# Two-block transformer layer on one core: global attention with unsplit values in the column halves and outputs kept transposed

## The reference, cut to what matters

```python
h = _rmsnorm(x, norm_gain[l])
q_a, k_a, v_a, g_a, q_b, k_b, v_b, g_b = jnp.split(h @ w_in[l], split_at, axis=-1)
...
sc = jnp.einsum('bqkgd,bskd->bkgqs', qi, k) * d ** -0.5      # 8 heads of 64, on 2 heads of keys and values
o_a = jnp.einsum('bkgqs,bskd->bqkgd', softmax(sc), v) * silu(g_a)
o_b = _neighbourhood_attn(q_b, k_b, v_b, na_rpb[l]) * silu(g_b)
x = x + jnp.concatenate([o_a, o_b], axis=-1) @ w_out[l]
```

## Time and profile before

| what | us |
|---|---|
| median of three runs | 2026.56 |
| the profiled execution's own time | 2022.47 |
| its span in the trace | 2020.7 |
| TensorE granted clock, mean | 0.989 |
| PE / DVE / ACT / POOL busy | 1900.6 / 1017.6 / 835.0 / 395.4 |
| attention a, first scores to first projection of attention b | 149.07 to 388.70 |
| attention b, pass 3 to the first matmul of wo1 | 636.9 to 672.95 |

### The profile page before, as it was taken

One profiled execution on the slowest core, in us unless ns is written; L12 is line 12 of the kernel. 1 busy time (PEld: TensorE's weight loads), 2 busy tenths in 40 slices (PEclk: granted clock), 3 DMA queues, 4 the chain that ended last, 5 costly groups with the idle time before them and its releaser, 6 DMA issues.

```text
span 2020.7 us, 39554 instructions
## 1 busy us (share of the span) xinstructions
PE 1900.6 (94%) x16369; PEld 1607.5 (80%) x16369; DVE 1017.6 (50%) x2372; ACT 835.0 (41%) x1812; POOL 395.4 (20%) x398
## 2 busy tenths in 40 slices
PE   6998899999999899989999999999999999999997
PEld 6987778888887799967777777777777788887897
DVE  4767778522444335024455544444444457775504
ACT  5336777533454324223333333334333254444423
POOL 2540000120122142222222222212112101002221
PEclk9999999999999999999999999999999999999999
DMA  5153300233323322322221122111122220004432
GB/s 177 43 176 78 83 22 1 79 92 119 108 88 102 126 74 76 109 87 62 71 75 59 54 67 66 57 59 56 56 67 62 71 58 22 22 11 156 157 136 84
DMA packets 148714, 159.96 MB, mean 79 GB/s; under 512 B 14932, under 2 KB 131992, under 8 KB 148536
## 3 DMA queue, kind: packets, MB, share of 16 engines
q1 hardware_dynamic: 148456, 156.97, 24.5%
q0 software_dynamic: 80, 0.47, 0.1%
HBM read 110.53 MB, written 52.62 MB: 81 GB/s over the span
## 4 chain that ended last, share of the span: by engine, by line
PE 70%; DVE 6%; ACT 4%; DMA 2%; issue 2%; POOL 2%; SPq 0%; DVEq 0%; POOLq 0%; ACTq 0%
PE ps L974 8%; PE ps L976 7%; PE ps L975 7%; PE ps L687 7%; PE ps L689 6%; PE ps L688 6%; PE ps L1077 4%; PE ps L1261 3%; PE ps L1284 3%; PE ps L1114 3%; PE ps L1143 2%; PE ps L1271 2%; PE ps L775 2%; PE ps L1063 1%; DMA t<-in_w_in 1%
## 5 line engine op out<-in xcount | busy, mean ns | idle before, releaser
L687 PE MATMUL ps<-t,t 128*128 128x256 f32 (+2 forms) x1392 | 434.7, 312 | 11.9 <-DVE t L2186 3.3
L688 PE MATMUL ps<-t,t 128*128 128x256 f32 (+2 forms) x1392 | 427.4, 307 | 0.0
L689 PE MATMUL ps<-t,t 128*128 128x256 f32 (+2 forms) x1392 | 427.3, 307 | 0.0
L2747 POOL TENSOR_TENSOR t<-t,t 128x512 fp32r<-128x512 f32 x183 | 237.3, 1310 | 949.7 <-ACT t L1362 949.7
L974 PE MATMUL ps<-t,t 128*128 128x512 f32 (+2 forms) x720 | 298.9, 415 | 0.8 <-ACT t L1647 0.8
L687 PEld LDWEIGHTS ps<-t,t 128*128 128x128 f32 x1392 | 268.6, 193 | 30.6 <-issue 14.4
L688 PEld LDWEIGHTS ps<-t,t 128*128 128x128 f32 x1392 | 268.8, 193 | 10.4 <-issue 0.2
L689 PEld LDWEIGHTS ps<-t,t 128*128 128x128 f32 x1392 | 268.3, 193 | 10.9
L976 PE MATMUL ps<-t,t 128*128 128x512 f32 (+2 forms) x720 | 269.6, 374 | 0.0
L975 PE MATMUL ps<-t,t 128*128 128x512 f32 (+2 forms) x720 | 269.3, 374 | 0.0
L1362 ACT ACTIVATE t<-t 128x512 fp32r<-128x512 f32 x186 | 110.1, 623 | 132.7 <-DMA t<-in_w_in 85.0
(11 more groups left out here) (262 smaller groups left out, 3212.8 us busy)
## 6 DMA issues: line engine op xcount, KB each, us to landing
t<-in_w_in SPq DMA_DIRECT2D x53, 512.0 KB, 5.8
zgate_spill<-t SPq DMA_DIRECT2D x20, 512.0 KB, 3.2
tile_bias<-t SPq DMA_DIRECT2D x16, 576.0 KB
t<-tile_bias SPq DMA_DIRECT2D x8, 1152.0 KB, 5.9
t<-in_x SPq DMA_DIRECT2D x16, 512.0 KB, 9.9
t<-zgate_spill SPq DMA_DIRECT2D x16, 512.0 KB, 3.7
feat_spill<-t SPq DMA_DIRECT2D x13, 512.0 KB, 3.3
t<-in_w_in SPq DMA_DIRECT2D x6, 1024.0 KB, 5.3
```

The lines of the kernel that those rows point to most:

```text
L687: e.matmul(dst, lh, rh, start=k == 0, stop=False)
L688: e.matmul(dst, lh, rl, start=False, stop=False)
L689: m = e.matmul(dst, ll, rh, start=False, stop=k == n - 1)
L2747: e.tensor_tensor(WLO[wslot(b)][:, o], WST[:, o], WHI[wslot(b)][:, o].bitcast(F), ALU.subtract).then_inc(w_lo.sem, w_lo.up((b, p)))
```

## The change

The items of global attention are ordered in fours: two heads by two tiles of queries. Values are no longer split: L767 of the new code multiplies the fp32 values (64 stationary columns of `QKV`) with unsplit fp32 probabilities, 256 columns of two tiles, head s in column half s. That is 16 fp32 matmuls for four items; they are issued in four parts of four, one behind each of the next four items. ACT copies one bank of turned probabilities, DVE the other. DVE multiplies the gates with 1/sum before (L2008), PE turns them (L771), ACT brings them to SBUF (`GTA`), and DVE multiplies the still transposed output with them (L2013). The result stays transposed and is written over the spent query columns of `QKV`. In pass 3 nothing is turned any more: ACT takes the high part straight from `QKV`, POOL the low part, and DVE (L2098, before ACT) takes the high part of the outputs of passes 0 to 2. Buffers of attention b move to other addresses. The banks of wo1 are written out. The second block is unchanged.

```diff
-        PTA = [[t_.rearrange("p (k c) -> p k c", c=256) for t_ in (hi_, lo_)]
-               for hi_, lo_ in ((sb([128, 2048], R, W0 + 72 * KB), sb([128, 2048], R, RW)), (WHI[0], WLO[0]))]
-        VHL = sb([128, 8, 768], R, W0 + 16 * KB)[:, :, 0:256].rearrange("p k (v s c) -> p k v s c", s=2, v=2)
-        OTA = sb([128, 256], F, W0 + 91 * KB)
+        PTA = [[sb([128, 8, 256], F, o) for o in two] for two in ((W0 + 72 * KB, RW), (RW + 8 * KB, RW + 24 * KB))]
+        GTA = sb([128, 256], F, W0 + 91 * KB)
...
-        MIXT = sb([128, 4, T], F, W0 + 16 * KB)
+        MIXT = sb([128, 4, T], F, W0)
+        GBP = [sb([128, 128], F, W0 + (18 + 3 * (t // 2)) * KB + 512 * (t % 2)) for t in range(NT)]
+        VGS = [sb([128, 256], F, W0 + (30 + 3 * i) * KB) for i in range(4)]
...
-        A_ITEMS = [(kv, h, i) for kv in range(2) for i in range(NT) for h in range(4)]
+        A_ITEMS = [(kv, 2 * g + s, 2 * i + j) for kv in range(2) for i in range(NT // 2) for g in range(2) for j in range(2) for s in range(2)]
...
+        def a_outputs(q):
+            kv, h, i = A_ITEMS[4 * q]
+            return i, tile128(2 * kv + h // 2)
+        def a_kept(n):
+            return PTA[n // 4 % 2][n % 2], tile128(n % 4 // 2)
+        def a_scored(i):
+            return 8 * (i // 2) + 5 + 2 * (i % 2)
...
+            def scores_a(n):
+                kv, h, i = A_ITEMS[n]
+                ps = [bank_at(("s", n, half), 2 * (n % 2) + half, (prob, n)) for half in range(2)]
...
                 for half in range(2):
+                    for x in range(2):
+                        m = e.matmul(ps[half], QT[:, h, tile128(i)], KTS[kv][:, x, half512(half)], start=x == 0, stop=x == 1)
+                m.then_inc(score_mm.sem, score_mm.up(n))
+            def turn_a(n):
+                w.wait_ge(*prob[n])
+                for half in range(2):
+                    ps = bank_at(("t", n, half), 4 + half, ((prob_hi, prob_lo)[half], (n, half)))
+                    for k in range(4):
+                        m = e.transpose(ps[:, tile128(k)], PB[n % 2][:, half512(half)][:, tile128(k)], ident)
+                    m.then_inc(prob_tr.sem, prob_tr.up((n, half)))
+            def value_a(q, part):
+                kv = A_ITEMS[4 * q][0]
+                i, channels = a_outputs(q)
+                ob = bank_at(("ot", q), 6, (attn_v, (q, "out"))) if part == 0 else banks[6]
+                w.wait_ge(*prob_hi[4 * q + 3, 0])
+                w.wait_ge(*prob_lo[4 * q + 3, 1])
+                w.wait_ge(*qkv_out[0, NT - 1])
+                for k in (2 * part, 2 * part + 1):
+                    for s in range(2):
+                        m = e.matmul(ob[64 * s:64 * s + 64, 0:256], QKV[:, k, 640 + 64 * kv:704 + 64 * kv], PTA[q % 2][s][:, k, :], start=k == 0, stop=k == 7)
+                if part == 3:
+                    w.wait_ge(*attn_v[q, "gates"])
+                    for j in range(2):
+                        m = e.transpose(ob[:, 256 + 128 * j:384 + 128 * j], MIXA[:, i + j, channels], ident)
+                    m.then_inc(value_mm.sem, value_mm.up(q))
+            for n in range(-1, 64 + 4):
                 i, step = n // 4, n % 4
+                if n + 1 < 64:
+                    scores_a(n + 1)
+                if 0 <= n < 64:
+                    turn_a(n)
+                if n >= 4:
+                    value_a(i - 1, step)
                 if n < 1:
                     t = n + 7
                     ps = bank_at(("ga", 1, t), t, (mixed_v, ("gate a", t)))
...
                 if 0 <= i < NT and step == 2:
-                    turn_head_keys(1, i, (6, 7))
-                elif 0 < i <= NT and step == 0:
-                    turn_head_queries(1, i - 1, (6, 7))
+                    turn_head_keys(1, i, (7,))
+                elif 1 < i <= NT + 1 and step == 0:
+                    turn_head_queries(1, i - 2, (7,))
...
-            def turn_mixed(i):
-                key = ("m", i, 0)
-                ps = bank_at(key, 7, (tile_hi, key), (tile_lo, key))
-                w.wait_ge(*attn_v[63, "out"])
...
             def output_product(n, i, ps, hi, lo):
+                w.wait_ge(*tile_hi["m", i])
                 w.wait_ge(*tile_hi["b", 3, i // 4])
                 w.wait_ge(*tile_lo["b", 3, i // 4])
-                w.wait_ge(*band_lo[2, 1])
+                w.wait_ge(*band_lo["m", NT - 1])
+                w.wait_ge(*band_lo["b", 2, 1])
...
-                    else:
-                        turn_mixed(n)
...
-                ps = bank_at(("wo1", 0, x), x, (resid_v, (0, x)))
+                ps = bank_at(("wo1", 0, x), (7, 0)[x], (resid_v, (0, x)))
...
-                    ps = bank(("wo1", n, i), ALL, (resid_v, (n, i)))
+                    ps = bank_at(("wo1", n, i), (i + 7) % 8, (resid_v, (n, i)))
...
+            w.wait_ge(*w_hi[5, 3])
+            w.wait_ge(*w_lo[5, 3])
+            for n in range(-1, 64 + 5):
+                if n >= 8 and step == 0:
+                    w.wait_ge(*value_mm[i - 2])
+                    if i > 2:
+                        w.wait_ge(*attn_v[i - 3, "out"])
+                    e.activation(GTA[:, :], psum(("ot", i - 2))[:, 256:512], ACT.Copy).then_inc(value_t.sem, value_t.up(i - 2))
+                if 0 <= n < 64:
+                    kept, tile = a_kept(n)
+                    if n > 7:
+                        w.wait_ge(*value_mm[i - 2])
+                    w.wait_ge(*prob_tr[n, 0])
+                    e.activation(kept[:, 0:4, tile], psum(("t", n, 0)).rearrange("p (k c) -> p k c", c=128), ACT.Copy).then_inc(prob_hi.sem, prob_hi.up((n, 0)))
+                if n + 1 < 64:
+                    z = n + 1
+                    w.wait_ge(*top[z])
+                    e.activation(PB[z % 2][:, :], ps_all[:, 1024 * (z % 2):1024 * (z % 2) + 1024], ACT.Exp, bias=NMX[:, z % 16:z % 16 + 1],
+                                 scale=1.0, accum_out=RSM[:, z % 16:z % 16 + 1]).then_inc(prob.sem, prob.up(z))
...
+                elif 0 < i <= NT and step == 3:
+                    split_queries(1, i - 1)
+                elif 1 < i <= NT + 1 and step == 0:
+                    head_queries(1, i - 2)
...
             def mixed_part(i):
+                w.wait_ge(*attn_v[15, "out"])
+                w.wait_ge(*dense_mm["q", 3, 1])
+                e.activation(AH[:, 0:4, tile128(i)], QKV[:, i, 0:512].rearrange("p (k c) -> p k c", c=128), ACT.Copy).then_inc(tile_hi.sem, tile_hi.up(("m", i)))
...
                         mixed_part(n)
-                        if n < len(MIXED):
-                            band_part(*MIXED[n])
                 if p < 3:
                     wt.leave()
             band_part(3, 0)
-            wt.enter()
             band_turned(B_Z + 31)
             for x in range(2):
-                wt.tick(12)
                 band_value(B_Z + 30 + x)
             band_part(3, 1)
+            wt.enter()
+            for _ in range(2):
+                wt.tick(12)
             ACTE.end("attention b")
 
...
+            def gates_a(q):
+                c = 4 * q % 16
+                i, channels = a_outputs(q)
+                g4 = MIXA[:, i:i + 2, channels].rearrange("p j (s c) -> p j s c", s=2)
+                w.wait_ge(*prob[4 * q + 3])
+                w.wait_ge(*gate_a[1, NT - 1])
+                e.reciprocal(RIN[:, c:c + 4], RSM[:, c:c + 4]).then_inc(attn_v.sem, attn_v.up((q, "sums")))
+                w.wait_ge(*attn_v[q, "sums"])
+                w.wait_ge(*mixed_v["gate a half", 7])
+                e.tensor_tensor(g4, g4, bc(RIN[:, c:c + 4].rearrange("p (j s) -> p j s", s=2), 3, 64), ALU.mult).then_inc(attn_v.sem, attn_v.up((q, "gates")))
+            def output_a(q):
+                i, channels = a_outputs(q)
+                w.wait_ge(*value_t[q])
+                e.tensor_tensor(QKV[:, i:i + 2, channels], psum(("ot", q))[:, 0:256].rearrange("p (j c) -> p j c", j=2), GTA[:, :].rearrange("p (j c) -> p j c", j=2),
+                                ALU.mult).then_inc(attn_v.sem, attn_v.up((q, "out")))
...
+            for n in range(-1, 64 + 5):
                 i, step = n // 4, n % 4
+                if n >= 8 and step == 0:
+                    output_a(i - 2)
+                if n + 1 < 64:
+                    z = n + 1
+                    w.wait_ge(*score_mm[z])
+                    maximum(ps_all[:, 1024 * (z % 2):1024 * (z % 2) + 1024], z)
...
+                if 0 <= n < 64:
+                    kept, tile = a_kept(n)
+                    if n > 7:
+                        w.wait_ge(*value_mm[i - 2])
+                    w.wait_ge(*prob_tr[n, 1])
+                    e.tensor_copy(kept[:, 4:8, tile], psum(("t", n, 1)).rearrange("p (k c) -> p k c", c=128)).then_inc(prob_lo.sem, prob_lo.up((n, 1)))
+                if n >= 4 and step == 0 and n <= 64:
+                    gates_a(i - 1)
...
+            def band_first(p, r):
+                w.wait_ge(*attn_v[B_Z + 8 * p + 4 * r + 3, "out"])
+                w.wait_ge(*dense_mm["q", 3, 1])
```

(21 more changed lines are left out.)

203 lines of the change are left out of this document (19 added, 184 removed).

## The result

| | before | after |
|---|---|---|
| median of the runs, us | 2024.69 (2022.34, 2022.83, 2026.56, 2026.66) | 1992.46 (1986.72, 1991.50, 1993.42, 1997.10) |
| profiled execution, us | 2022.47 | 1991.50 |
| its span, us; mean granted clock | 2020.7; 0.989 | 1989.7; 0.990 |

After to before is 0.984, with a 95% interval of 0.981 to 0.987: faster by 32.2 us in the medians and by 31.0 in the profiled executions. The forecast was 1992, with 1981 to 2009 as its range.

A forecast was written before the change was run, and what follows sets the result against it. PE together with ACT's two serial copies was taken to bound attention a. Savings of 23 + 6 + 3 = 32 us gave 1990.5 from the profiled 2022.47 and 1994.6 from 2026.56; forecast 1992, between them, range 1981 to 2009.

The forecast's parts named there:

- 23 + 6 + 3 = 32 us: Forecast savings: 23 us in attention a, 6 in pass 3 of attention b, 3 in the output projection.
- The slot: Attention a, value part: time of two 256-column records, one in each column half, taken as 0.22 us, four per part.
- Going into and out of the shape: Attention a: cost of the 64-column shape per value part, 0.17 us within it plus 0.20 on the instruction behind.
- The lower bound of 2.9 us for an item: Attention a, steady loop: least time of one item without any cost of the shape; 3.11 us was forecast.
- The cover sum of the prediction: Attention a: maximum, exponential and handovers, 2.6 us, fit under 3.06 us of PE's transposes, value part and scores.
- The end: Attention a from the last scores' start: 9.3 us instead of 11.2, so 1.9 saved, with PE going on without waiting.
- Covered, with 1 us per tile to spare: Pass 3: POOL's eight more subtractions fit, two per tile taking 2.5 of 3.5 us.
- the 3 us either way: Output projection's start: allowance for whether the low clock behind pass 3, costing about 3 us, stays.
- (b): Rival, attention a: late handover of bank 6 or probabilities costs each four items 1 us, 16 us, 2008; chance 0.1.
- (d): Rival: pass 3 and output projection gains never reach the end, POOL or clock taking back 9 us, 2001; chance 0.1.
- (c): Rival, attention a value parts: column halves run one behind the other, 56 us more, 2048, slower; chance 0.03.
- (a): Rival, attention a value parts: column halves overlap only in part, slot 0.275 us, 14 us more, 2006; chance 0.12.

The follow-up runs named there:

- e_onehalf: Changed kernel with both heads' value matmuls sent to the same column half and added up there: 2046.27 us.
- e_ahead: Changed kernel with scores made two items ahead and eight value matmuls in a row behind every second item: 1979.92 us, 0.977 of the kernel before.
- e_actboth: Changed kernel with ACT making both copies of the turned probabilities and DVE none: 1991.44 us.
- e_v8: Changed kernel with eight value matmuls in a row behind every second item: 2004.12 us.
- e_v16: Changed kernel with all sixteen value matmuls of a group in a row behind the fourth item: 2008.81 us.
- e_p3dve: Changed kernel with the low part of the global outputs in pass 3 made by DVE again instead of POOL: 2002.11 us.
- e_p3early: Changed kernel with ACT making the high part of the global outputs one tile earlier in pass 3: 1990.31 us.
- e_banks: Kernel before with only the written-out banks of the output projection: 2023.01 us against 2026.93, 0.9983.
- e_grouped: Changed kernel with the four matmuls of a value part issued head by head instead of by turns: 1992.49 us.
- e_best: e_ahead and e_p3early together, on the changed kernel: 1981.52 us, 0.977 of the kernel before.

## Why the prediction was right

**Sum and total.** 23 + 6 + 3 = 32 us were forecast, and the stages that the change touches lost 24.9 + 6.4 + 3.0 = 34.3. The total met the forecast closer than its terms deserve: a gain of 2.7 us in pass 0 that no term has, 0.5 in pass 1, and losses of 1.2 in pass 2 and 4.6 in the untouched rest cancel the surplus. That is luck. The 6.4 us of pass 3 are the upper end, too: in the eight other kernels that leave the pass as the change made it, it took 30.2 to 31.6 us, so 4.5 to 6.4 are gained there.

**Slot and change of shape.** The slot was taken as 0.22 us and is 0.212 to 0.216 (e_onehalf, by the stage and by the starts of records): the lower bound, 2 x 107 ns, was the right one, with full overlap. Going into and out of the shape was taken as 0.17 + 0.20 = 0.37; it is 1.01 - 4 x 0.21 = 0.17 within the part and 1.12 - 0.93 = 0.19 on the scores behind. Fewer changes gave 0.34 each in e_ahead. The four items came out at 12.23 us instead of 12.45 in the second half, and at 12.8 in most of the first instead of 13.1: eight and seven times 0.2 to 0.3 are 3.9 us, twice the 1.9 us by which attention a beat its term; the end took 1.6 us of them back. (The lower bound of 2.9 us for an item without any cost of the shape is a slip: 0.93 + 0.88 + 4 x 0.213 + 0.055 is 2.7. Nothing else rests on it.)

**What the rows of before meant.** The prediction read the earlier trace rows as PE together with ACT's two copies in series, and expected the loop to become PE's because ACT loses a copy. The outcome was right and this reason was not. With both copies on ACT (e_actboth) nothing is lost, and with one copy but the value matmuls in rows of eight (e_v8) the pair is back at 6.65 us. The decisive thing is cover: sixteen value matmuls stood behind one item of a pair, none behind the other, and spreading them is worth 14.2 of the 24.9 us. Not shown is what the spread alone would have done in the kernel before, with two copies and two subtractions to an item; no run has its sixteen split matmuls spread out. The cover sum of the prediction, 2.6 us of chain under 3.06 us of PE's work, is the part that held, and 1.25 of the 3.06 is the value part. Its spare 0.5 us was right to the sign: with one exception of 0.5 us there are no waits in the steady loop.

**The price of the shape.** The prediction called 64 changes at 0.37 what speaks against the change, with the rule of the Trainium skill that a change of tiling mode drains the array (TensorEngine Tiling (Array Packing), Key Properties); the rows agree, about 0.35 a part, 22 us in all. Whoever had saved them by longer rows, though, would have lost 14 to 17 us (e_v8, e_v16). They can be saved only with scores further ahead, and then only by half.

**Start and end of attention a.** The start was expected 2 us shorter and is 1.9 (scores 4 come 18.1 us behind the first instead of 20.0), and the wait of L831 is gone. The end was expected 1.9 us shorter, 9.3 us, and takes 11.0 instead of 11.2: 0.3. The sum had PE going on without a wait there. It waited 0.67 us for ACT's last exponential, and 0.93 for DVE's output of the group before, which frees bank 6; DVE's copy of the last probabilities had ended 1.6 us earlier.

**Pass 3.** A tile was forecast at 3.5 us and takes 3.24 to 3.67. e_p3dve shows that ACT's copy in DVE's chain was the limit, as assumed: with it back, a tile takes 4.29 us. The pass lost twice my estimate, because POOL beside DVE or a half-clock spell made it 4.94 in others. Behind the last scores of the pass, only 0.2 us were gained (7.64 to 7.48). "Covered, with 1 us per tile to spare" was wrong by a little: POOL's last subtraction doubles DVE's last, 0.65 us on the path (e_p3early).

**Output projection.** -2.9 forecast, -3.0 found, and the bank edit alone takes the wait away (e_banks). The half clock behind pass 3 stayed, 0.76 over the first 11.4 us of the projection against 0.74, so the 3 us either way that I kept for it went neither way.

**Rivals.** (b) came once, 0.93 us at the end of attention a, and not in every group of four, for which it had 16 us. (d) did not come: pass 3 and the output projection kept 9.4 us. (c) is out by e_onehalf. (a) had the figure of the Trainium skill for three column tiles behind it (TensorE: Matmul & The Clock Gate, Part 3: Packing small matmuls); for two halves of 64 columns with 256 fp32 columns each the measured overlap is 1.87 / 1.01, and without the 0.17 for the shape 1.70 / 0.84 = 2.0.

## What to carry to other kernels

When a chain of waits shows another engine's work between pieces of PE, first ask whether PE's own work is spread so that every step of the chain has some beside it; moving an operation to another engine may then be needless. Small pieces have a price, here 0.35 us per change of the matmul's shape, and two levers trade against each other: pieces short enough to cover each link, and enough items in flight that pieces can be longer. Scores two items ahead gave 11 us of attention a that way on top of the change. A last group has no next one to cover it: look at the end of a loop by itself.

## What the runs showed of the hardware that I had not expected

- A subtraction or product of DVE with both operands in SBUF does not end before one of POOL's that is under way: 128x512 takes 0.69 us alone and up to 1.41 beside POOL (e_p3dve), 128x128 takes 0.29 alone and up to 1.38. In the changed kernel's timeline:
```profile
623.05 1.27 POOL L2743 TENSOR_TENSOR t<-t,t 128x512 fp32r<-128x512 f32 x1
```
```profile
623.64 0.83 DVE L2087 TENSOR_TENSOR t<-t,t 128x128 f32<-128x128 f32 x1
```
POOL's ends at 624.32 and DVE's at 624.47, 0.15 behind it. All six of this form that met one of POOL's in pass 3 ended 0.15 behind it, whenever they began; those of 128x512 ended 0.54 to 0.58 behind it. DVE's operations of 128x384 that read PSUM stayed at 0.54 to 0.55. The Trainium skill says so (SBUF — State Buffer, SBUF: two separate sides): the pair of ports that the two share goes to whichever starts first for its whole instruction, when DVE's has two SBUF inputs. The rows agree, and the prediction left this rule out, though the change gives POOL eight more instructions right beside DVE's chain; it costs DVE 0.5 to 1.1 us in three tiles of pass 3. A cast from SBUF to SBUF, with one operand, can stand still as well: in e_p3early one begun at 617.80, 0.11 behind POOL's, took 1.49 us instead of 0.42. And POOL can be the one that waits: its subtraction at 618.02 in the changed kernel, 0.06 behind the start of a cast of DVE's, took 1.48 us instead of 1.27.
- The order of matmuls for the two column halves did not matter over a group of four: 1.02 us for the part against 1.01 (e_grouped).
- The spread between runs of one kernel, here 10 us, goes with the mean granted clock, from 0.991 at 1986.72 us to 0.986 at 1997.10. The rest of the program, not touched, differs by 3.1 us between the profiles of e_ahead and e_best, with 10 us more at the half clock in the longer one.
